# S5 scan: GpSimd instead of VectorE takes the whole turns from the phases

## The chip, the cores and the metric

The kernel runs on one core of one Trainium2 chip. The metric is the device time of one execution in microseconds (us), from the hardware. Engines are named TensorE (PE in the profile, its weight loads PEld), VectorE (DVE), ScalarE (ACT), GpSimd (POOL) and SyncE (SP).

## The reference, cut to what matters

The program is a two-layer backbone: in layer 0 grouped-query attention beside a gated recurrent scan, in layer 1 latent attention beside an S5 diagonal state-space model, and in each layer a mixer that picks and weighs experts. The change touches only the S5 part of layer 1:

```python
for d in range(2):                                   # forward, backward
    lam  = lax.complex(a_re[d], a_im[d])
    dt   = jnp.exp(log_dt[d])[:, None]
    abar = jnp.exp(lam * dt)                         # complex decay, one per state
    ...
    h_ctx = _diag_scan(abar, einsum('btgc,gpc->btgp', fl(ucg), bbar), None)
    h_lat = _diag_scan(abar, einsum('btgc,gpc->btgp', fl(u), bbar), h_ctx[:, -1])
    y = y + fl(einsum('gcp,btgp->btgc', cmat, h_lat).real)
```

There are 256 context positions and 512 latent positions, so each scan is over 768 positions, for 32 groups of 64 states in two directions. All of it is float32.

## The kernel before, in words

Each stage of the kernel is a block of its own, with one instruction stream per engine, and a stage begins when the one before has ended on all engines. The S5 scan (`stage_s5_scan`, L2321 to L2505) handles 128 states at a time: 32 units in all, one for each of 16 pairs of groups and each direction, forward and backward by turns.

The complex scan is made of two real ones. The input of every position is turned back by the angle that the state has run through up to there, then a scan with the real decay (`rate`) alone runs over the real and the imaginary part, and the result is turned forward again. For that a unit needs a sine and a cosine of 768 angles in each of 128 partitions. The steps of unit n, by engine:

- **ScalarE**, `phases(n)`, L2401 and L2404: the time index times the unit's turns per step gives `phase`; the same plus a large constant (`ROUND`, 1.5 times two to the 23rd) gives `whole`, which is the phase rounded to a whole number with the constant still on it. `phase` has two buffers, `whole` has one. ScalarE calls `phases(n+1)` ahead of the sine and cosine of unit n; it first waits until phase n is finished, since only then `whole` is free, and until the cosine of unit n-1 has been read from the other buffer.
- **VectorE**, `phases(n)`, L2441: one instruction, (`whole` - ROUND) - `phase`, leaves the fraction of a turn in `phase`, with its sign turned. It is issued for unit n+1 ahead of the work on unit n.
- **ScalarE**, L2418 to L2423: sine, cosine of half the angle, its square, and the cosine from it. Ahead of them it waits for the finished phase, and (from the third unit on) for the products of unit n-2, since `sin` and `cos` have two buffers.
- **TensorE**, L2364: eight matmuls put the unit's real and imaginary input into PSUM. They start when VectorE has read the input of the unit before (L2468).
- **VectorE**, L2463 to L2466: four products of `sin` or `cos` (SBUF) with the inputs (PSUM); L2469 and L2470: two sums, all operands in SBUF; then the scans over `v` with the broadcast `rate`: L2478 twice on 768 columns in a forward unit, L2480 twice on 256 and L2486 twice on 512 in a backward one.
- **GpSimd**, L2504: four products of the scan's result with `cos` or `sin` over the 512 latent positions, all in SBUF, once the scans of the unit have ended.
- **TensorE**, L2376: eight matmul records take these products to the output in PSUM; after every eight units VectorE reads a quarter of it (L2447).

Beside this ScalarE, TensorE and SyncE work off a piece of the modulation weights in each unit (L130 to L161), which needs neither VectorE nor GpSimd. SyncE issues one load per unit for that. GpSimd issues no transfer in this stage.

The order on each engine is the written one, and semaphores count the units: `phase_rounded` (ScalarE has written `whole`), `phase_ready` (the fraction is there), `trig_ready`, `bu_ready`, `scanned`, `prods_ready`, `y_ready`.

Of the kernel before, what the change touches and what calls it, by code (L numbers as in the profile page):

```python
# [17 lines left out]
ALU = mybir.AluOpType  # L18
# [2148 lines left out]
ROUND = 1.5 * 2.0 ** 23  # L2167
# [153 lines left out]
def stage_s5_scan(nc, g, u_t, rate, turns, b_t, c_t, z_t, later):  # L2321
# [5 lines left out]
    units = [(j, i, d) for j in range(4) for i in range(4) for d in range(2)]  # L2327
    with ExitStack() as stack:
        a = Arena(nc, stack)
        tau = a.sb("tau", [P, 2, T])  # L2330
        phase = a.sb("phase", [P, 2, T])
        whole = a.sb("whole", [P, T])
# [5 lines left out]
        prods = a.sb("prods", [P, 2, 4, LAT])  # L2338
        to_whole = a.sb("to_whole", [P, 1])
        (loaded, rounding_ready, phase_made, phase_rounded, phase_ready, half_ready, sq_ready, trig_ready, bu_ready, bu_used, scanned, prods_ready, y_ready,  # L2340
         y_read, own_v, phase_used, d_added) = a.sem(
            "loaded", "rounding_ready", "phase_made", "phase_rounded", "phase_ready", "half_ready", "sq_ready", "trig_ready", "bu_ready", "bu_used", "scanned",
            "prods_ready", "y_ready", "y_read", "own_v", "phase_used", "d_added")
        mod = ModPiece(a, g, later, [a.sb("ada_ring", [P, DK, P])], 4 * BANK, 5 * BANK, P)
        block = a.block()
        ps = g.ps
# [2 lines left out]
        @block.sync  # L2349
        def _(sp):  # L2350
            sp.dma_start(tau[:], g.d["k_s5_tau"]).then_inc(loaded, 16)
            for j in range(mod.n):
                mod.load(sp, j)
# [78 lines left out]
        @block.vector  # L2432
        def _(dve):
            mod.clear(nc, dve)
            own = Steps(dve, own_v)
            tt = nc.vector.tensor_tensor

            def phases(n):

                dve.wait_ge(phase_rounded, n + 1)  # L2440
                nc.vector.scalar_tensor_tensor(out=phase[:, n % 2], in0=whole[:], scalar=ROUND, in1=phase[:, n % 2],  # L2441
                                               op0=ALU.subtract, op1=ALU.subtract).then_inc(phase_ready, 1)

            def readout(j):
                dve.wait_ge(y_ready, 8 * (j + 1))
                at = VEC["s5_d"][0] + j
                nc.vector.scalar_tensor_tensor(out=z_t[:, j], in0=u_t[:, j, CTX:T], scalar=g.vec[:, at:at + 1],  # L2447
                                               in1=ps[:, YB + (j % 2) * BANK:YB + (j % 2 + 1) * BANK],
                                               op0=ALU.mult, op1=ALU.add).then_inc(y_read, 1)
                dve.wait_ge(y_read, j + 1)  # L2450
                dve.sem_inc(d_added, 1)

            nc.vector.memset(to_whole[:], ROUND).then_inc(rounding_ready, 1)
            phases(0)
            for n, (j, i, d) in enumerate(units):
                unit = d * S5_TILES + 4 * j + i
                b = n % 2
                if n + 1 < len(units):
                    phases(n + 1)
                re, im = ps[:, BU:BU + T], ps[:, BU + 1024:BU + 1024 + T]  # L2460
                dve.wait_ge(trig_ready, n + 1)
                dve.wait_ge(bu_ready, n + 1)
                own(tt(v[:, 0], cos[:, b], re, ALU.mult))  # L2463
                own(tt(x2[:, 0], sin[:, b], im, ALU.mult))
                own(tt(v[:, 1], cos[:, b], im, ALU.mult))
                own(tt(x2[:, 1], sin[:, b], re, ALU.mult))  # L2466
                own.settle()
                dve.sem_inc(bu_used, 1)  # L2468
                own(tt(v[:, 0], v[:, 0], x2[:, 0], ALU.add))  # L2469
                own(tt(v[:, 1], v[:, 1], x2[:, 1], ALU.subtract))  # L2470
                own.settle()
                if n >= 2:
                    dve.wait_ge(prods_ready, n - 1)
                r = rate[:, unit:unit + 1]
                for part in range(2):
                    x, out = v[:, part], s[:, b, part]
                    if d == 0:
                        own(nc.vector.tensor_tensor_scan(out, r.to_broadcast([P, T]), x, 0.0, ALU.mult, ALU.add))  # L2478
                    else:
                        own(nc.vector.tensor_tensor_scan(out[:, 0:CTX][:, ::-1], r.to_broadcast([P, CTX]),  # L2480
                                                         x[:, 0:CTX][:, ::-1], 0.0, ALU.mult, ALU.add))
                if d == 1:
                    own.settle()
                    for part in range(2):
                        x, out = v[:, part], s[:, b, part]
                        own(nc.vector.tensor_tensor_scan(out[:, CTX:T][:, ::-1], r.to_broadcast([P, LAT]),  # L2486
                                                         x[:, CTX:T][:, ::-1], out[:, 0:1], ALU.mult, ALU.add))
                own.settle()
                dve.sem_inc(scanned, 1)  # L2489
                if i == 0 and d == 1 and j:  # L2490
                    readout(j - 1)
            readout(3)
            mod.keep(nc, dve)

        @block.gpsimd
        def _(pool):
            for n in range(len(units)):
                b = n % 2
                pool.wait_ge(scanned, n + 1)
                pool.wait_ge(trig_ready, n + 1)  # L2500
                if n >= 2:
                    pool.wait_ge(y_ready, n - 1)
                for c, (part, table) in enumerate(((0, cos), (1, sin), (0, sin), (1, cos))):
                    last = nc.gpsimd.tensor_tensor(prods[:, b, c], s[:, b, part, CTX:T], table[:, b, CTX:T], ALU.mult)  # L2504
                last.then_inc(prods_ready, 1)  # L2505
# [186 lines left out]
def layer_odd(nc, g, until):  # L2692
    w_in = g.d["od_w_in"][0].rearrange("(k p) n -> p k n", p=P)
    with ExitStack() as stack:
        a = Arena(nc, stack)
        y_t = a.sb("y_t", [P, DK, LAT])
        with ExitStack() as inner:
# [35 lines left out]
            if until >= 9:  # L2733
                N = 2 * S5_TILES
                z_t = y_t[:, 4:DK]
                with ExitStack() as scope:
                    c = Arena(nc, scope)
                    rate = c.sb("rate", [P, N])
                    turns = c.sb("turns", [P, N])
                    b_t = c.sb("b_t", [P, 2, N, P])  # L2740
                    c_t = c.sb("c_t", [P, 3, N, P])
                    stage_s5_parameters(nc, g, rate, turns, b_t, c_t)
                    stage_s5_scan(nc, g, u_t, rate, turns, b_t, c_t, z_t, [(1, u) for u in range(16, 48)])
                w = b.sb("w_out_odd", [P, DK, D])
                w_out = g.d["od_w_out"][0]
                rows = [(slice(0, P), k, w_out[k * P:(k + 1) * P, :]) for k in range(DK)]
                stage_s5_glu(nc, g, z_t, w, rows)
                if until >= 10:
                    stage_mix_out(nc, g, 1, y_t, CTX, w)
# [60 lines left out]
```

## Time and profile before

| what | us |
|---|---|
| runs of the kernel before, median of 3 | 5373.76 |
| lowest and highest of them | 5368.46 and 5385.42 |
| the profiled execution, its own time | 5372.74 |
| its span in the profile | 5370.9 |
| the whole kernel: PE, DVE, ACT, POOL busy | 4356.5, 3626.4, 1193.6, 1541.8 |
| stretch 3380 to 3757 us (this stage), DVE busy | 348.07 of 377 |
| the same stretch, POOL busy | 180.10 of 377 |

The profile gives one execution; its own time is 1.8 us above its span (what lies around the first and last instruction). The shares of the whole kernel are averages over stages with different limits; this stage is about 7% of the span and is read by itself. The granted TensorE clock was 0.86 of full speed in it.

### The profile page before, as it was taken

To read this page: it belongs to the slowest core of one execution; us is meant where nothing else is said; L and a number is where in the kernel's file an instruction comes from. 1 tells how busy PE (TensorE), PEld (TensorE's weight loads), DVE (VectorE), ACT (ScalarE), POOL (GpSimd) and SP (SyncE) were. 2 spreads that over 40 slices of the span, in tenths; PEclk is the share of its full clock that TensorE was granted. 3 is DMA by queue.
4 is the path that set the end of the run, shared out by engine and by line. 5 is a ranking of instruction groups with operands and counts; after the bars stand their busy time and mean duration, and the time that the engine had idled before them with its cause. 6 is when DMAs were issued, how large, how long until landed. Compare 5 with 4: busy or idle time off the path is not lost. (4 is left out here: it accounts for less than half of the span.)

```text
span 5370.9 us, 58089 instructions
## 1 busy us (share of the span) xinstructions
PE 4356.5 (81%) x21260; PEld 3212.1 (60%) x21260; DVE 3626.4 (68%) x6899; ACT 1193.6 (22%) x1919; POOL 1541.8 (29%) x1488
## 2 busy tenths in 40 slices
PE   6976787989999995788788676677689998967886
PEld 5854786865666663454455434333577887856765
DVE  3146764249989887688788534898339988735665
ACT  2125222122232221000000224544223333300000
POOL 0000330004333545344444000354003334333441
PEclk8988898999999997899899878888899999988987
DMA  4211002149888999999999100111238999999996
GB/s 158 63 65 67 1 5 79 48 179 332 284 277 311 413 395 386 366 394 393 378 389 392 54 18 9 42 47 44 79 131 311 315 340 395 366 361 402 403 403 238
DMA packets 465030, 1252.88 MB, mean 233 GB/s; under 512 B 52054, under 2 KB 186956, under 8 KB 459116
## 3 DMA queue, kind: packets, MB, share of 16 engines
q0 software_dynamic: 184320, 671.17, 32.7%
q1 hardware_dynamic: 275984, 569.51, 29.1%
q10 hardware_dynamic: 4444, 8.48, 0.4%
q8 instruction: 171, 2.80, 0.2%
q14 instruction: 111, 0.91, 0.1%
HBM read 1146.24 MB, written 102.76 MB: 233 GB/s over the span
## 5 line engine op out<-in xcount | busy, mean ns | idle before, releaser
L1898 PE MATMUL banks<-acts_in,v_rows 128*128 128x384 f32 (+1 forms) x4096 | 1160.1, 447 | 304.0 <-DMA v_rows<-peer_v 157.2
L1553 PE MATMUL banks<-h_dense,u_t 128*128 128x384 f32 (+1 forms) x4096 | 1216.0, 441 | 0.0
L1898 PEld LDWEIGHTS banks<-acts_in,v_rows 128*128 128x128 f32 x4096 | 798.5, 197 | 665.3 <-DMA v_rows<-peer_v 173.4
L1527 POOL DMA_INDIRECT rows<-peer_u,expert x640 | 655.0, 1024 | 1538.7 <-DVE weight L1798 833.4
L1553 PEld LDWEIGHTS banks<-h_dense,u_t 128*128 128x128 f32 x4096 | 757.1, 195 | 252.0 <-issue 12.2
L1880 POOL DMA_INDIRECT v_fetched<-peer_v,expert x640 | 607.2, 949 | 861.8 <-DVE banks L1958 709.4
L1798 DVE CUSTOM_DVE_ANT_0 rows<-rows,banks 128x1024 f32<-128x1024 f32 x640 | 762.1, 1214 | 128.1 <-DMA rows<-peer_u,expert 80.4
L1958 DVE SCALAR_TENSOR_TENSOR banks<-v_fetched,weight,banks 128x1024 f32<-128x1024 f32 x630 | 784.7, 1283 | 0.0
L1936 DVE TENSOR_TENSOR acts_in<-acts_in,gates 128x384 f32<-128x384 f32 (+1 forms) x256 | 125.1, 489 | 405.1 <-DMA acts_in<-activations 404.9
L1544 PE MATMUL banks<-ident,u_raw 128*128 128x128 f32 x2048 | 319.6, 280 | 82.8 <-DMA u_raw<-peer_u 82.4
L1611 ACT COPY u_t<-banks 128x512 f32<-128x512 f32 x512 | 300.7, 588 | 338.2 <-PE banks L1544 333.8
L1544 PEld LDWEIGHTS banks<-ident,u_raw 128*128 128x128 f32 x2048 | 253.8, 145 | 174.4 <-DMA u_raw<-peer_u 108.2
L1889 ACT COPY y_tok<-banks 128x1024 f32<-128x1024 f32 x5 | 5.1, 1012 | 1460.6 <-DVE banks L1958 1460.6
L2504 POOL TENSOR_TENSOR prods<-s,cos 128x512 f32<-128x512 f32 x64 | 81.0, 1266 | 622.0 <-DVEq L2489 622.0
L1585 PEld LDWEIGHTS banks<-gate_hot,first_hot 128*128 128x128 f32 x1280 | 176.3, 203 | 80.7 <-issue 52.3
L1585 PE MATMUL banks<-gate_hot,first_hot 128*128 128x128 f32 x1280 | 180.5, 288 | 50.6 <-DVE gate_hot L1781 50.6
L2364 PE MATMUL banks<-u_t,b_t 128*128 128x512 f32 (+1 forms) x256 | 128.2, 661 | 106.4 <-DVEq L2468 105.4
L1010 POOL TENSOR_TENSOR z<-expo,keep_k 128x384 f32<-128x384 f32 x28 | 30.8, 1106 | 596.9 <-ACT expo L986 596.9
L1618 ACT ACTIVATE acts<-banks 128x384 f32<-128x384 f32 (+1 forms) x256 | 111.8, 437 | 382.1 <-PE banks L1553 382.0
L1634 ACT COPY part<-banks 128x512 f32<-128x512 f32 x160 | 93.6, 585 | 437.3 <-PE banks L1585 437.3
L1781 DVE TENSOR_SCALAR gate_hot<-iota,slots 128x128 f32<-128x128 f32 x640 | 177.9, 360 | 0.0
L1942 DVE SCALAR_TENSOR_TENSOR x_t<-banks,mod,x_t 128x384 f32<-128x384 f32 (+1 forms) x264 | 160.0, 609 | 0.0
(398 smaller groups left out, 6199.4 us busy)
## 6 DMA issues: line engine op xcount, KB each, us to landing
u_raw<-peer_u SPq DMA_DIRECT2D x256, 512.0 KB, 6.6
v_rows<-peer_v SPq DMA_DIRECT2D x256, 512.0 KB, 15.2
gate_table<-part SPq DMA_DIRECT2D x20, 2048.0 KB, 11.9
activations<-acts SPq DMA_DIRECT2D x128, 192.0 KB
gates<-gate_table SPq DMA_DIRECT2D x8, 3072.0 KB, 22.5
acts_in<-activations SPq DMA_DIRECT2D x128, 192.0 KB, 11.3
peer_wq_in<-peer_wq SPq DMA_DIRECT2D x16, 1024.0 KB, 5.8
ada_ring<-ada_w SPq DMA_DIRECT2D x32, 512.0 KB, 3.8
```

What stands on the lines that cost most here:

```text
L1527: pool.indirect_dma_start(out=ring[:, s % U_RING, :], out_offset=None, in_=rows_of_u, in_offset=bass.IndirectOffsetOnAxis(ap=expert[:, t, ...
L1544: last = nc.tensor.transpose(ps[:, TURN + c:TURN + c + P], u_raw[:, i % 2, c:c + P], g.ident[:])
L1553: last = nc.tensor.matmul(out, u_t[:, i % 2, k * P:(k + 1) * P], h[:, k], start=(k == 0), stop=(k == DK - 1))
L1585: last = nc.tensor.matmul(out[:, j * P:(j + 1) * P], first_hot[:, q % HOTS, j], gate_hot[:, q % HOTS, j], start=True, stop=True)
L1611: nc.scalar.copy(u_t[:, i % 2, c:c + BANK], ps[:, TURN + c:TURN + c + BANK]).then_inc(ut_ready, 1)
L1781: last = nc.vector.tensor_scalar(gate_hot[:, b, j], iota[:], slots[:, 1, c + j:c + j + 1], slots[:, 2, c + j:c + j + 1], ALU.is_equal, ALU ...
L1798: nc.vector.tensor_tensor_reduce(out=row, in0=row, in1=ps[:, H:H + D], scale=1.0, scalar=0.0, op0=ALU.mult, op1=ALU.add, accum_out=weight[ ...
L1880: pool.indirect_dma_start(out=ring[:, s % V_RING, :], out_offset=None, in_=rows_of_v, in_offset=bass.IndirectOffsetOnAxis(ap=expert[:, t, ...
L1898: return nc.tensor.matmul(y_at(m if RESIDENT else j // GROUP * DK + m), v[:, j % V_ROWS, m * P:(m + 1) * P], acts[:, j % V_ROWS], start=st ...
L1942: nc.vector.scalar_tensor_tensor(out=x, in0=y_at(u), scalar=g.mod[:, layer, 40 + m, stream:stream + 1], in1=x, op0=ALU.mult, op1=ALU.add). ...
L1958: last = nc.vector.scalar_tensor_tensor(out=acc(k % 2), in0=row, scalar=weight[:, t, k:k + 1], in1=acc(k % 2), op0=ALU.mult, op1=ALU.add)
L2364: last = nc.tensor.matmul(ps[:, BU + part * 1024 + lo:BU + part * 1024 + hi], b_t[:, part, unit], u_t[:, j, lo:hi], start=True, stop=True)
```

## The change

GpSimd calls `phases` in place of VectorE. Its form has two instructions: a subtraction of the constant from `whole` in place, a wait for that to have landed, and the difference of `whole` and `phase`. GpSimd calls it for units 0 and 1 at the start, and for unit n+2 ahead of its wait for the scans of unit n. VectorE's instruction and its wait for `phase_rounded` are gone. A semaphore that nothing used gives its place to the one of GpSimd's new wait.

```diff
@@ stage_s5_scan
-         y_read, own_v, phase_used, d_added) = a.sem(
+         y_read, own_v, own_p, d_added) = a.sem(
...
@@ block.vector
-            def phases(n):
-
-                dve.wait_ge(phase_rounded, n + 1)
-                nc.vector.scalar_tensor_tensor(out=phase[:, n % 2], in0=whole[:], scalar=ROUND, in1=phase[:, n % 2],
-                                               op0=ALU.subtract, op1=ALU.subtract).then_inc(phase_ready, 1)
-
...
-            phases(0)
             for n, (j, i, d) in enumerate(units):
                 unit = d * S5_TILES + 4 * j + i
                 b = n % 2
-                if n + 1 < len(units):
-                    phases(n + 1)
...
@@ block.gpsimd
+            def phases(n):
+                pool.wait_ge(phase_rounded, n + 1)
+                nc.gpsimd.tensor_scalar(whole[:], whole[:], ROUND, None, ALU.subtract).then_inc(own_p, 1)
+                pool.wait_ge(own_p, n + 1)
+                nc.gpsimd.tensor_tensor(phase[:, n % 2], whole[:], phase[:, n % 2], ALU.subtract)\
+                    .then_inc(phase_ready, 1)
+
+            phases(0)
+            phases(1)
             for n in range(len(units)):
                 b = n % 2
+                if n + 2 < len(units):
+                    phases(n + 2)
                 pool.wait_ge(scanned, n + 1)
```

## Rows read from the trace of the kernel before

**Rows 1.** Page head; 335 us: PE, PEld, DVE, ACT, POOL busy, clock, DMA, GB/s.

```profile
span 5370.9 us, 58089 instructions
...
3400.00:3735.00 335.00, 242.77 (x1007) 119.52 (x1006) 324.19 (x302) 158.11 (x206) 170.22 (x120) 0.88 0.16 48
```

**Rows 2.** Groups by line, 3360 to 3780 us: busy, mean ns | idle before, releasers.

```profile
L2504 POOL TENSOR_TENSOR prods<-s,sin 128x512 f32<-128x512 f32 x64 | 101.7, 1607 | 0.0
L2504 POOL TENSOR_TENSOR prods<-s,cos 128x512 f32<-128x512 f32 x64 | 81.0, 1266 | 622.0 <-DVEq L2489 622.0
...
L2441 DVE SCALAR_TENSOR_TENSOR phase<-whole,phase 128x768 f32<-128x768 f32 x32 | 61.3, 1916 | 12.3 <-ACT whole L2404 7.9
L2478 DVE TENSOR_TENSOR_SCAN s<-rate,v 128x768 f32<-128x768 f32 x32 | 54.5, 1745 | 0.6
...
L2486 DVE TENSOR_TENSOR_SCAN s<-rate,s,v 128x512 f32<-128x512 f32 x32 | 39.4, 1272 | 0.6
...
L2463 DVE TENSOR_TENSOR v<-cos,banks 128x768 f32<-128x768 f32 x32 | 30.1, 942 | 2.6 <-ACT cos L2423 2.3 <-PE banks L2364 0.3
...
L2421 ACT ACTIVATE cos<-cos 128x768 f32<-128x768 f32 x32 | 27.0, 843 | 1.0
...
L2480 DVE TENSOR_TENSOR_SCAN s<-rate,v 128x256 f32<-128x256 f32 x32 | 20.4, 679 | 0.6
```

**Rows 3.** Waits of the same stretch: us in total, times, longest.

```profile
PE banks L2364 <- DVEq L2468: 105.4, 31, 13.2
```

**Rows 4.** Timeline, GpSimd, one unit: start us, us, engine, line.

```profile
3513.65 1.27 POOL L2504 TENSOR_TENSOR prods<-s,cos 128x512 f32<-128x512 f32 x1 [5.42 <-DVEq L2489]
3514.87 3.23 POOL L2504 TENSOR_TENSOR prods<-s,sin 128x512 f32<-128x512 f32 x2
3518.06 1.27 POOL L2504 TENSOR_TENSOR prods<-s,cos 128x512 f32<-128x512 f32 x1
```

**Rows 5.** Timeline, VectorE, the same unit, and the start two units on.

```profile
3513.66 2.07 DVE L2441 SCALAR_TENSOR_TENSOR phase<-whole,phase 128x768 f32<-128x768 f32 x1
3515.65 0.94 DVE L2463 TENSOR_TENSOR v<-cos,banks 128x768 f32<-128x768 f32 x1
...
3518.25 0.94 DVE L2466 TENSOR_TENSOR x<-sin,banks 128x768 f32<-128x768 f32 x1
3519.34 0.96 DVE L2469 TENSOR_TENSOR v<-v,x 128x768 f32<-128x768 f32 x1
3520.21 0.95 DVE L2470 TENSOR_TENSOR v<-v,x 128x768 f32<-128x768 f32 x1
...
3536.20 2.07 DVE L2441 SCALAR_TENSOR_TENSOR phase<-whole,phase 128x768 f32<-128x768 f32 x1
```

**Rows 6.** Timeline of the last unit, which has no L2441 before it.

```profile
3739.08 1.27 POOL L2504 TENSOR_TENSOR prods<-s,cos 128x512 f32<-128x512 f32 x1 [5.43 <-DVEq L2489]
3739.24 0.95 DVE L2463 TENSOR_TENSOR v<-cos,banks 128x768 f32<-128x768 f32 x1 [0.30 <-PE banks L2364]
...
3742.78 1.26 POOL L2504 TENSOR_TENSOR prods<-s,cos 128x512 f32<-128x512 f32 x1
3742.94 1.92 DVE L2469 TENSOR_TENSOR v<-v,x 128x768 f32<-128x768 f32 x1
```

**Rows 7.** One stage of layer 0: VectorE and GpSimd, two SBUF inputs each.

```profile
582.58 2.13 POOL L1013 TENSOR_TENSOR hg<-expo,hg 128x768 f32<-128x768 f32 x1
...
583.53 2.00 DVE L1044 TENSOR_TENSOR expo<-cum 128x768 f32<-128x768 f32 x1
```

**Rows 8.** Lines L1010, L1017: duration ns min/median/max, first and last start, forms.

```profile
L1010 POOL TENSOR_TENSOR z<-expo,keep_k x28: 979/1002/1532, 535.7 to 740.9; 128x384 f32<-128x384 f32 x28
...
L1017 POOL TENSOR_TENSOR k_dec<-expo,keep_k x8: 1799/1800/1801, 554.5 to 782.2; 128x768 f32<-128x768 f32 x8
```

**Rows 9.** The stage's start: the first phases on VectorE.

```profile
3385.69 0.96 DVE L2441 SCALAR_TENSOR_TENSOR phase<-whole,phase 128x768 f32<-128x768 f32 x1 [5.92 <-ACT whole L2404]
3388.62 0.96 DVE L2441 SCALAR_TENSOR_TENSOR phase<-whole,phase 128x768 f32<-128x768 f32 x1 [1.97 <-ACT whole L2404]
3391.84 0.95 DVE L2463 TENSOR_TENSOR v<-cos,banks 128x768 f32<-128x768 f32 x1 [2.26 <-ACT cos L2423]
```

More of the change, by code:

```diff
@@ L2340, in stage_s5_scan @@
         (loaded, rounding_ready, phase_made, phase_rounded, phase_ready, half_ready, sq_ready, trig_ready, bu_ready, bu_used, scanned, prods_ready, y_ready,
-         y_read, own_v, phase_used, d_added) = a.sem(
+         y_read, own_v, own_p, d_added) = a.sem(
             "loaded", "rounding_ready", "phase_made", "phase_rounded", "phase_ready", "half_ready", "sq_ready", "trig_ready", "bu_ready", "bu_used", "scanned",
-            "prods_ready", "y_ready", "y_read", "own_v", "phase_used", "d_added")
+            "prods_ready", "y_ready", "y_read", "own_v", "own_p", "d_added")
         mod = ModPiece(a, g, later, [a.sb("ada_ring", [P, DK, P])], 4 * BANK, 5 * BANK, P)
```

## The prediction

> **What bounds the kernel now.** Stages follow one another, so what this stage gains or loses goes into the time unshortened. I read the page first for the span, then the busy times of the stage's steady stretch. There VectorE is busy 324 of 335 us, GpSimd 170, ScalarE 158 and TensorE 243 [rows 1]: the stage looks bound by VectorE. The groups by line agree: VectorE waited 2.6 us in all ahead of L2463, the first use of sine, cosine and inputs, and TensorE waited 105 us for VectorE to give its inputs free [rows 2, 3]. By this reading the change takes a 2 us step off the bound and should gain.
>
> The timeline shows what the busy times hide. L2441 has a record of 2.07 us beside GpSimd's first product, but 0.96 us at the start of the stage, where GpSimd is idle [rows 5, 9]. GpSimd's next two products take 3.23 us where two others take about 2 x 1.23 [rows 4, 6]. So the two engines did not run side by side: GpSimd's first product (3513.65, 1.23 us to the next start), then VectorE's L2441 (about 0.87), and only then GpSimd's second. In the last unit L2469 comes 0.16 us after the start of GpSimd's fourth product and takes 1.92 us instead of 0.96 [rows 5, 6]. In layer 0 a VectorE instruction of 768 columns with both operands in SBUF takes 2.00 us beside a GpSimd product [rows 7]. But L2463 and L2466, which read one operand from PSUM, keep 0.94 us while GpSimd works [rows 4, 5]. What these rows have in common: a VectorE instruction with two SBUF inputs and a GpSimd product exclude each other for their whole length. I call what they share the port.
>
> The port's load per unit before is: four products of 1.23 us (3739.08 to 3742.78 is three of them [rows 6]), 4.93; L2441, 0.87 (the spacing of three such instructions from 3515.65 to 3518.25 [rows 5]); L2469 and L2470, 1.74; and the scans, if they need it too, (54.5 + 39.4 + 20.4) / 32 = 3.57 [rows 2]. The sum is 11.11 us. A unit takes (3536.20 - 3513.66) / 2 = 11.27 us [rows 5]. The port would be taken all the time but 0.16 us, and VectorE's busy time of 324 us contains its waits for it.
>
> **Does a scan need the port?** No row has a scan beside a GpSimd instruction: GpSimd's products end at about 3519.3, where L2469 begins, and return only when the scans are over [rows 4, 5]. A scan reads two tensors from SBUF, `v` and the broadcast `rate`, so it belongs by its operands with L2441, L2469 and L1044, which were held up, and not with L2463. I take it that it needs the port. The Trainium skill states this for such operands (SBUF — State Buffer, Who interferes with whom): a VectorE instruction with two SBUF inputs contends with a GpSimd instruction that reads SBUF, and the later one waits for the whole of the other. By that rule the time is my forecast; with the scans exempt it is one of the first two rivals.
>
> **The change part by part.**
> - Removed from VectorE: L2441, a slot of 1.99 us (3513.66 to 3515.65 [rows 5]), of which 0.87 is its own port time and the rest is waiting for a product that GpSimd has to do anyway. Of the 32 slots, those for units 2 to 31 lie between two units. The first two lie in ScalarE's lead at the start [rows 9].
> - Added to GpSimd, second instruction: a difference of two tensors of 768 columns. L1017 is exactly that: 1.80 us [rows 8].
> - Added to GpSimd, first instruction: one tensor less a constant, 768 columns. No row shows this on GpSimd. From 384 to 768 columns a product with two inputs goes from 1.00 to 1.80 us [rows 8], so 0.20 is fixed and 1.60 is for 768 columns of two inputs. With one input I take half: 0.20 + 0.80 = 1.00 us. Low end: 0.84 us, what ScalarE takes for 768 columns of one input [rows 2]. High end: 1.80 us, the second input costing nothing. A gain is excluded, since the instruction is new. The Trainium skill (GPSIMD Engine Reference, Engine selection) says one-input work on GpSimd runs roughly at line rate and two-input work about twice as slow; at its 1.2 GHz that is 0.64 + 0.20 = 0.84 us, which would take 5 us off the sum.
> - The wait between the two (own_p): some 0.1 us, during which VectorE has the port; it costs only at the start. Behind it stand the unit's products, and TensorE's output and ScalarE's sine of two units on behind these.
> - "Two units ahead" gives no lead by itself. ScalarE writes `whole` for unit n+2 only after phase n+1 is finished, as before. But by the time GpSimd is through with the products of unit n-1 it has done so, hence GpSimd's wait for it costs nothing. No transfer moves.
>
> **Where it lies in a unit.** Scans of a unit end; GpSimd starts its four products and VectorE its four instructions on PSUM, which need no port. Then L2469, L2470 and the scans, 5.3 us, meet the rest of the products and the new pair, and each waits for the other in turn. VectorE's scans are the end of the chain, so all of it adds up: 4.93 + 1.74 + 3.57 + 1.00 + 1.80 = 13.04, and the same 0.16 us of handing over: 13.20 us per unit against 11.27, **1.93 us more**. It is the same as 1.00 + 1.80 - 0.87: the port carries 2.80 us of new work for 0.87 of old.
>
> **The sum.** In units 1 to 29 a phase pair and four products lie beside VectorE's work: 29 x 1.93 = 56.0. In unit 0 only the pair does; one wait for its first instruction, 1.0. Unit 30 has lost L2441 and has no pair any more: it gives back 1.99 and waits for one product, 1.24: -0.8. At the start the first phase takes 1.00 + 0.1 + 1.80 instead of 0.96, and ScalarE's next step waits for it: +1.9. Unit 31 stays as it is. In all +58.1 us. The profiled execution took 5372.74, its span 5370.9; that gives 5430.8. The median of the runs is 1.0 us above it, and I take **5431**.
>
> What covers the rest, and is late next: sine and cosine of unit n+2 begin after the products of unit n, some 6 us into a unit, take about 3.4 us (four steps like L2421 [rows 2]) and are done before 10, so they stay hidden in 13.2 us. TensorE waited 105 us over 31 units, 3.4 each [rows 3], and waits longer.
>
> **Rivals.**
> - **Scans don't need the port, L2469 goes ahead of the fourth product (faster).** This is the case on the other side. Then the pair runs beside the scans for nothing. VectorE's unit is 11.27 - 1.99 = 9.28, and it waits for one product of 1.24 in front of L2469 or L2470: 10.52, or 0.75 less per unit. 29 x -0.75, with start, unit 0 and unit 30 (1.9 + 1.0 - 0.8): -20, 5354. It decides if a scan keeps its 1.75 us while GpSimd works. For it: scans are another kind of instruction, at half the speed, and no row holds one beside GpSimd. Against: their operands.
> - **Scans don't need it, the fourth product goes first.** L2469 is ready 3.69 us after VectorE's first product (3515.65 to 3519.34), the fourth product starts 3.70 after GpSimd's first [rows 5, 6], a tie. If the product wins, L2469 waits 1.24 and L2470 waits 1.00 for the new subtraction: 9.28 + 2.24 = 11.52, 0.25 more, 29 x 0.25 + 2.1 = +9: 5383, no difference that counts. In my forecast the tie changes nothing, since all the work has to pass the port.
> - **GpSimd's subtraction costs as much as two inputs.** The port carries 0.80 more: 58 + 30 x 0.80 = +82: 5456.
> - **The busy times are right after all**, L2441's slot falls away and nothing comes for it: 30 x -1.99 = -60, 5314. Against it stands the last unit, the one without L2441 already: its L2469 took 0.96 longer [rows 6].
>
> **How the numbers follow.** A measurement of this kernel can tell about 0.3%, 16 us, from no change. Chances: forecast with the subtraction anywhere from 0.84 to 1.5 us, 0.77; subtraction at about 1.80 or more, 0.08; scans free and faster by 20 us, 0.09; scans free and about level, 0.05; the full gain, 0.01. So faster 0.10, same 0.05, slower 0.85. The range takes the port case: at the low end 0.16 x 30 = 5 us less for the subtraction and about as much again if the handing over of 0.16 a unit goes, 5420, and 3 us for the spread of runs: 5417. At the high end the price of 1.80 gives 5456. The two cases with free scans are left out, 15 in 100.
>
> **What would show it.** L2441 is gone; GpSimd has 32 subtractions of about 1.0 us and 32 differences of 1.8 us or, where they waited, more. L2478, L2480 and L2486 rise: their sum goes from 114 us to about 114 + 30 x 2.8 less what falls to L2470, so L2478's mean is well over 2 us. L2470 and L2469 together wait about 1.2 us or more per unit. VectorE still looks busy over 90% of the stage, its distance from unit to unit is about 13.2 us, and the stage is 58 us longer. I am wrong if L2478 keeps 1.75 us with a GpSimd record beside it; then the unit is 10.5 to 11.5 us. If the scans wait and the time still is elsewhere, it is the subtraction's own length.

## The result and the profile after

The changed kernel took 5414.91 us (median of 4 runs, 5413.85 to 5433.23) where the kernel before took 5376.95 in the runs beside it (5368.46 to 5385.42). The ratio is 1.0076, 95% interval 1.0059 to 1.0092: slower by 38 us, clear of noise. I had forecast 5431, +58 us. The direction and the mechanism held. My +58 us is half as large again as the +38 us measured, and the median lies 2 us below the low end of my range, 5417.

Line numbers move: L2463 is now L2454, L2469 and L2470 are L2460 and L2461, the scans L2478, L2480, L2486 are L2469, L2471, L2477, and GpSimd's products L2504 are L2506. New are L2490 (GpSimd's subtraction of the constant) and L2492 (its difference). The page's head and the same 335 us of the stage, which answer to [rows 1]:

```profile
span 5413.3 us, 58123 instructions
...
3400.00:3735.00 335.00, 242.57 (x905) 117.29 (x906) 323.37 (x242) 143.94 (x188) 265.25 (x159) 0.81 0.15 43
```

VectorE is busy for 323 of 335 us, as before (324), and gets through fewer instructions in them (242 against 302). The granted TensorE clock was 0.81 of full speed here against 0.88. VectorE waited for TensorE only once in this stage, 10.5 us at its end, and before it was 11.5 us in the same place, so the clock is not where the time went.

VectorE's and GpSimd's groups of the stage (line, engine, operation, tiles, shapes, count | busy us, mean ns | idle before, releasers), which answer to [rows 2]:

```profile
L2490 POOL TENSOR_SCALAR whole<-whole 128x768 f32<-128x768 f32 x32 | 88.7, 2772 | 434.3 <-ACT whole L2404 434.3
...
L2469 DVE TENSOR_TENSOR_SCAN s<-rate,v 128x768 f32<-128x768 f32 x32 | 77.9, 2477 | 0.5
L2492 POOL TENSOR_TENSOR phase<-whole,phase 128x768 f32<-128x768 f32 x32 | 72.3, 2260 | 2.7
...
L2460 DVE TENSOR_TENSOR v<-v,x 128x768 f32<-128x768 f32 x32 | 59.5, 1860 | 4.7
L2461 DVE TENSOR_TENSOR v<-v,x 128x768 f32<-128x768 f32 x32 | 48.4, 1513 | 0.0
...
L2471 DVE TENSOR_TENSOR_SCAN s<-rate,v 128x256 f32<-128x256 f32 x32 | 44.8, 1442 | 0.5
L2477 DVE TENSOR_TENSOR_SCAN s<-rate,s,v 128x512 f32<-128x512 f32 x32 | 39.4, 1272 | 0.6
L2454 DVE TENSOR_TENSOR v<-cos,banks 128x768 f32<-128x768 f32 x32 | 30.5, 954 | 22.4 <-ACT cos L2423 15.2 <-DVE s L2469 3.9 <-DVE s L2477 2.7
```

The two sums before, which [rows 2] leave out:

```profile
L2469 DVE TENSOR_TENSOR v<-v,x 128x768 f32<-128x768 f32 x32 | 31.6, 988 | 4.7
L2470 DVE TENSOR_TENSOR v<-v,x 128x768 f32<-128x768 f32 x32 | 30.4, 952 | 0.0
```

L2441's 61.3 us [rows 2] are gone from VectorE, and still it is as busy: the two sums and the scans took 176.3 us and now take 270.0, 93.7 more. Their work is the same as before; I read the growth as waiting for the port, and the timeline below shows it. L2454, which reads one operand from PSUM, has kept its length. Apart from the 15.2 us at the start, nothing of VectorE's idle time grew by more than 0.22 us a unit.

One forward unit, VectorE and then GpSimd, from the timeline:

```profile
3499.14 1.99 DVE L2460 TENSOR_TENSOR v<-v,x 128x768 f32<-128x768 f32 x1
3501.05 1.57 DVE L2461 TENSOR_TENSOR v<-v,x 128x768 f32<-128x768 f32 x1
3502.66 4.97 DVE L2469 TENSOR_TENSOR_SCAN s<-rate,v 128x768 f32<-128x768 f32 x2
...
3511.55 1.99 DVE L2460 TENSOR_TENSOR v<-v,x 128x768 f32<-128x768 f32 x1
```

```profile
3499.05 1.27 POOL L2506 TENSOR_TENSOR prods<-s,cos 128x512 f32<-128x512 f32 x1
3500.28 2.84 POOL L2490 TENSOR_SCALAR whole<-whole 128x768 f32<-128x768 f32 x1
3503.20 2.82 POOL L2492 TENSOR_TENSOR phase<-whole,phase 128x768 f32<-128x768 f32 x1
3507.77 1.27 POOL L2506 TENSOR_TENSOR prods<-s,cos 128x512 f32<-128x512 f32 x1 [1.75 <-DVEq L2480]
```

Read it as one queue for the port. L2460 comes 0.09 us behind the fourth product and waits for it (1.99 instead of 0.96). GpSimd's subtraction then waits for L2460. L2461 waits for the subtraction, 1.57 instead of 0.95: 0.62 us. The difference, L2492, waits for the first scan (2.82 instead of 1.81), and the second scan waits for the difference: the pair takes 4.97 instead of 3.41. The shortest, the median and the longest of the single scans show that one of a pair waits and the other does not:

```profile
L2469 DVE TENSOR_TENSOR_SCAN s<-rate,v x32: 1728/1760/3308, 3401.8 to 3781.3; 128x768 f32<-128x768 f32 x32
```

So **a scan does need the port**: it waits for GpSimd's difference, and the difference waits for a scan. The trace of before had no row on this. From one L2460 to the next are 12.41 us. GpSimd then idles 1.75 us until the scans end, so it is not the bound by its own load.

What was mis-sized shows at the start of the stage, where VectorE has nothing to do yet:

```profile
3387.08 2.13 POOL L2490 TENSOR_SCALAR whole<-whole 128x768 f32<-128x768 f32 x1 [430.27 <-ACT whole L2404]
3389.29 1.80 POOL L2492 TENSOR_TENSOR phase<-whole,phase 128x768 f32<-128x768 f32 x1
3393.11 2.13 POOL L2490 TENSOR_SCALAR whole<-whole 128x768 f32<-128x768 f32 x1 [2.02 <-ACT whole L2404]
```

The subtraction alone takes 2.13 us, longer than the difference of two tensors, and above the 1.80 that I had as its high end. Yet it keeps VectorE waiting for 0.62 us only. I call this wait the hold. It is counted from the start of the waiting instruction, so the true hold can be a few hundredths of a us longer.

**Where the 42 us are.** The profiled execution took 5415.21 us, 42.5 more than that of before. From the first to the last L2463 (now L2454), 31 units, it was 3391.84 to 3739.24 before [rows 6, 9], 347.4 us, and is now:

```profile
L2454 DVE TENSOR_TENSOR v<-cos,banks x32: 953/954/956, 3396.3 to 3783.6; 128x768 f32<-128x768 f32 x32
```

387.3 us, so 39.9 more, or as an average of the 31 units 12.49 us against 11.21. The two ends of the stage are in this average. Between them a forward and a backward unit together take 25.22 us, 12.61 each, against 11.27 before [rows 5]:

```profile
3734.97 0.95 DVE L2454 TENSOR_TENSOR v<-cos,banks 128x768 f32<-128x768 f32 x1 [0.22 <-DVE s L2469]
...
3747.79 0.95 DVE L2454 TENSOR_TENSOR v<-cos,banks 128x768 f32<-128x768 f32 x1 [0.22 <-DVE s L2477]
...
3760.19 0.95 DVE L2454 TENSOR_TENSOR v<-cos,banks 128x768 f32<-128x768 f32 x1 [0.22 <-DVE s L2469]
```

The units 1 to 29, counted from one L2454 to the next, make 39.0 of the 39.9 us, or 1.345 each; units 0 and 30 together make the other 0.9. The first phases at the start take 3.1 more: the first L2463 came 12.29 us after the stage's first VectorE instruction (3379.55), L2454 comes 15.39 after it (3380.88). The stages ahead make 1.3 us and what lies behind the last L2454 makes -1.9. The average between first and last start is the measure of each experiment below, called "a unit" there.

### The profile page after: what moved, and what is told of

Same layout as the page of the kernel before. It is cut to its first block and busy times, and to the rows that moved or that the text cites. A ratio compares the mean times of both kernels' runs of the same rounds, so it can differ in the third digit from the quotient of the medians.

```text
span 5413.3 us, 58123 instructions
## 1 busy us (share of the span) xinstructions
PE 4365.0 (81%) x21260; PEld 3208.7 (59%) x21260; DVE 3660.3 (68%) x6867; ACT 1193.0 (22%) x1919; POOL 1680.8 (31%) x1552
## 5 line engine op out<-in xcount | busy, mean ns | idle before, releaser
L2364 PE MATMUL banks<-u_t,b_t 128*128 128x512 f32 (+1 forms) x256 | 149.6, 754 | 125.9 <-DVEq L2459 125.0
L2490 POOL TENSOR_SCALAR whole<-whole 128x768 f32<-128x768 f32 x32 | 88.7, 2772 | 434.3 <-ACT whole L2404 434.3
L1010 POOL TENSOR_TENSOR z<-expo,keep_k 128x384 f32<-128x384 f32 x28 | 30.8, 1105 | 598.0 <-ACT expo L986 598.0
L2364 PEld LDWEIGHTS banks<-u_t,b_t 128*128 128x128 f32 x256 | 71.3, 292 | 190.8 <-DVEq L2459 128.3
```

Of the source, the lines that this page charges most:

```text
L2364: last = nc.tensor.matmul(ps[:, BU + part * 1024 + lo:BU + part * 1024 + hi], b_t[:, part, unit], u_t[:, j, lo:hi], start=True, stop=True)
```

## The experiments

**Does GpSimd's work beside the scans cost VectorE time, and by what?** Three runs put one spare GpSimd instruction into the kernel before, where the change has its pair, and differ in it alone.

```diff
             for n in range(len(units)):
                 b = n % 2
+                if n >= 2:
+                    pool.wait_ge(y_ready, n - 1)
+                spare = prods[:, b].rearrange("p c t -> p (c t)")[:, 0:T]
+                if n:
+                    nc.gpsimd.tensor_tensor(spare, tau[:, 0], tau[:, 1], ALU.mult).then_inc(phase_used, 1)    # e1
+                    nc.gpsimd.tensor_scalar(spare, tau[:, 0], 2.0, None, ALU.subtract).then_inc(phase_used, 1)  # e2
+                    nc.gpsimd.memset(spare, 0.0).then_inc(phase_used, 1)                                        # e3
                 pool.wait_ge(scanned, n + 1)
                 pool.wait_ge(trig_ready, n + 1)
-                if n >= 2:
-                    pool.wait_ge(y_ready, n - 1)
+                if n:
+                    pool.wait_ge(phase_used, n)
```

> The kernel before, with one more GpSimd instruction in each of 31 units, after the four products: the product of two constant tensors of 768 columns, written where the next products will overwrite it. Nobody waits for it. Port theory (VectorE instructions with two SBUF inputs, scans among them, and GpSimd instructions that read SBUF exclude each other): L2470 and the scans are held by about 1.6 us per unit, as the first scan pair was in the changed kernel, so 31 x 1.6 = +50 us; L2478 or L2480 rise. Rival 'scans are free': it runs beside the scans, at most L2470 is held, +0 to 10 us.

> As the run before, but the spare instruction subtracts a constant from one tensor of 768 columns. Its record should be 2.13 us, as that of the changed kernel beside nothing. Port theory with the hold read from the changed kernel (VectorE was held 0.62 us by an instruction of 2.13 us): 31 x 0.65 = +20 us. Rival 'the record's whole length is what VectorE waits for': 31 x 2.1 = +66 us, more than the difference costs. By my prediction's price of 1.00: +31 us.

> As the run before, but the spare instruction only writes: a memset of 768 columns. Port theory for reads: nothing is held, 0 us within 0.1%, records of L2470 and the scans as before. Rival 'any GpSimd work in this place holds VectorE': its record's length of under 1 us per unit, up to +25 us.

The product of two tensors gave 1.0093 (1.0070 to 1.0117), +50 us; the subtraction 1.0034 (1.0022 to 1.0045), +18 us; the memset 1.0004 (0.9993 to 1.0015), nothing. From the groups by line, e1, e2 and e3 in turn:

```profile
L2469 DVE TENSOR_TENSOR v<-v,x 128x768 f32<-128x768 f32 x32 | 80.3, 2509 | 4.7
...
L2503 POOL TENSOR_TENSOR prods<-tau 128x768 f32<-128x768 f32 x31 | 56.9, 1836 | 0.0
```

```profile
L2503 POOL TENSOR_SCALAR prods<-tau 128x768 f32<-128x768 f32 x31 | 85.9, 2770 | 0.1
...
L2469 DVE TENSOR_TENSOR v<-v,x 128x768 f32<-128x768 f32 x32 | 61.5, 1922 | 4.7
...
L2470 DVE TENSOR_TENSOR v<-v,x 128x768 f32<-128x768 f32 x32 | 47.8, 1494 | 0.0
...
L2441 DVE SCALAR_TENSOR_TENSOR phase<-whole,phase 128x768 f32<-128x768 f32 x32 | 32.4, 1013 | 12.4 <-ACT whole L2404 8.0
```

```profile
L2469 DVE TENSOR_TENSOR v<-v,x 128x768 f32<-128x768 f32 x32 | 31.7, 990 | 4.7
L2470 DVE TENSOR_TENSOR v<-v,x 128x768 f32<-128x768 f32 x32 | 30.4, 951 | 0.0
...
L2503 POOL MEMSET prods<- 128x768 f32 x31 | 22.8, 737 | 0.0
```

A record of 1.84 us costs 50 us and one of 2.77 us costs 18, so the length of GpSimd's record is not what VectorE pays. In e3, GpSimd writes 768 columns beside L2469 in each unit, and L2469 keeps its 0.99 us: this write alone held nobody up. In e1 the hold fell on L2469, not on L2470 and the scans as I had written. In e2 L2469 is longer too (1.92 against 0.99), but that is an old wait in a new place: L2441 got the port ahead of GpSimd's first product there and fell from 1.92 to 1.01 us, and L2469 waited for the fourth product instead. What is new is the 0.54 us more on L2470. The scans kept their length in all three runs, so these runs do not bear on whether a scan needs the port; the timeline of the changed kernel does. Per unit (first to last L2463): 12.77 us in e1, 11.78 in e2, 11.20 in e3, against 11.21.

**What was L2441 worth?**

```diff
-                dve.wait_ge(phase_rounded, n + 1)
-                nc.vector.scalar_tensor_tensor(out=phase[:, n % 2], in0=whole[:], scalar=ROUND, in1=phase[:, n % 2],
-                                               op0=ALU.subtract, op1=ALU.subtract).then_inc(phase_ready, 1)
+                pass
...
-                    act.wait_ge(phase_ready, n)
+                    act.wait_ge(phase_rounded, n)
...
-                act.wait_ge(phase_ready, n + 1)
+                act.wait_ge(phase_rounded, n + 1)
```

> Leaves out the subtraction of the whole turns altogether (sine and cosine are taken of the unreduced phase); ScalarE still writes both tensors. It prices what the change took from VectorE. Port theory: of L2441's slot of 1.99 us the 0.87 of its own goes, the wait for a product moves to L2469 or L2470 (last unit of the kernel before: 0.96): 30 x -0.9 = -27 us. Rival 'VectorE's busy time is the bound': 30 x -1.99 = -60 us.

0.9947 (0.9926 to 0.9968), -26 us by the medians (5350.50 against 5376.40); 10.37 us a unit. The sine and cosine are then taken of the unreduced phase, so this is a price and not a kernel to keep. It is the most that taking L2441 off VectorE could bring with all else left as it is, since nothing is put in its place. Of its slot of 1.99 us the port part goes and the wait for a product moves to the next instruction on the port (now L2467):

```profile
L2467 DVE TENSOR_TENSOR v<-v,x 128x768 f32<-128x768 f32 x32 | 59.8, 1868 | 4.7
```

**Is it a matter of where L2441 waits?** The kernel before, with `phases(n + 1)` called behind the first product instead of ahead of it:

```diff
-                if n + 1 < len(units):
-                    phases(n + 1)
...
                 own(tt(v[:, 0], cos[:, b], re, ALU.mult))
+                if n + 1 < len(units):
+                    phases(n + 1)
                 own(tt(x2[:, 0], sin[:, b], im, ALU.mult))
```

> The kernel before with L2441 issued behind L2463 instead of ahead of it, nothing else. It then reaches the port 0.87 us into GpSimd's first product and its wait of 1.1 us shrinks to about 0.2. Rival 'what bounds is the wait in that one place': 30 x -0.85 = -25 us. Port theory: the port was taken already for 11.1 of 11.27 us; GpSimd's products still end late and L2469 waits for the fourth instead, so the time stays within 0.2% of the kernel before.

1.0002 (0.9993 to 1.0012). L2441's mean falls from 1.92 to 1.14 us and L2469's rises from 0.99 to 1.59:

```profile
L2469 DVE TENSOR_TENSOR v<-v,x 128x768 f32<-128x768 f32 x32 | 50.9, 1589 | 4.7
...
L2441 DVE SCALAR_TENSOR_TENSOR phase<-whole,phase 128x768 f32<-128x768 f32 x32 | 36.6, 1144 | 6.0 <-ACT whole L2404 6.0
```

Of a wait of 0.77 us that was taken away in one place, 0.60 came back in another, and a unit takes 11.13 us where it took 11.21. This is how a shared resource that is almost full looks.

**The changed kernel without GpSimd's subtraction.** ScalarE takes the constant off.

```diff
-                nc.scalar.activation(whole[:], phase[:, n % 2], ACT.Identity, bias=to_whole[:])\
-                    .then_inc(phase_rounded, 1)
+                nc.scalar.activation(whole[:], phase[:, n % 2], ACT.Identity, bias=to_whole[:]).then_inc(own_p, 1)
+                act.wait_ge(own_p, n + 1)
+                nc.scalar.activation(whole[:], whole[:], ACT.Copy, bias=-ROUND).then_inc(phase_rounded, 1)
...
-                nc.gpsimd.tensor_scalar(whole[:], whole[:], ROUND, None, ALU.subtract).then_inc(own_p, 1)
-                pool.wait_ge(own_p, n + 1)
```

> The changed kernel, but ScalarE takes the constant off `whole` (one more ScalarE instruction per unit, about 0.9 us, with 0.1 us of its own wait), and GpSimd only forms the difference. Port theory with the measured holds: GpSimd's subtraction held VectorE 0.62 us per unit, so 30 x 0.62 = 19 us off the changed kernel, and 2 to 3 us off its start: about 5394 where the changed kernel has 5415, and still 18 us above the kernel before, because a difference of about 1.6 us on the port stands for VectorE's 0.87. Rival 'the subtraction's 2.13 us record is in the chain': 60 us off, below the kernel before.

1.0049 (1.0035 to 1.0064) of the kernel before, 5398.58 against 5372.66 us: 11.91 us a unit, 18.1 us over 31 units below the changed kernel and 21.8 above the kernel before. The subtraction's share is 0.58 us a unit, not 2.13. What is left is the difference, which holds VectorE's L2462 (the former L2470) for 2.57 - 0.95 = 1.62 us where VectorE's own instruction took 0.87 of the port. GpSimd and VectorE, from the timeline of this run:

```profile
3543.20 2.53 POOL L2491 TENSOR_TENSOR phase<-whole,phase 128x768 f32<-128x768 f32 x1
```

```profile
3543.98 2.57 DVE L2462 TENSOR_TENSOR v<-v,x 128x768 f32<-128x768 f32 x1
```

**The pair ahead of the products.**

```diff
-                if n + 2 < len(units):
-                    phases(n + 2)
                 pool.wait_ge(scanned, n + 1)
+                if n + 2 < len(units):
+                    phases(n + 2)
                 pool.wait_ge(trig_ready, n + 1)
```

> The changed kernel with GpSimd's pair ahead of the four products of a unit instead of behind them: the same instructions in another order. The rival that only the sum of the holds on the port counts expects the time of the changed kernel within 0.2%. My reading is that the port is held 0.62 us of the subtraction's 2.13 us; ahead of the products GpSimd wastes the rest of it in the 3.5 us in which VectorE needs no port, and the products then fall beside L2469, L2470 and the scans. Per unit: pair until 4.0 us, the products from there; about 1 us more than now, 25 to 40 us above the changed kernel.

1.0155 (1.0137 to 1.0172): 13.75 us a unit, 39 us over the changed kernel. The same instructions in another order take longer, so the sum of the holds alone does not set the time. My reading was that a pair in the stretch in which VectorE wants no port wastes that stretch. This run does not show it by itself: the products now end so late that ScalarE's sine and cosine come late as well, a wait that I had called covered. Waits of this run, in total, times, longest:

```profile
DVE v L2454 <- ACT cos L2423: 73.2, 17, 15.1
```

Without the 15.1 at the start these are 16 waits of 3.6 us, 58 us in all, which is more than the 39 us lost. How much of the loss is wasted port time and how much is late sine and cosine stays open. The order in the change, pair behind products, is the better of the two.

**Taking load off the port.** If the port bounds, VectorE's instruction should be made to use one SBUF operand. In e7, 512 of the 768 columns of `whole` lie in PSUM; in e9, all of them, for which the output has one bank instead of two.

```diff
# e7
-        whole = a.sb("whole", [P, T])
+        whole = a.sb("whole", [P, 256])
...
+        whole_ps = ps[:, 3 * BANK:4 * BANK]
...
-                nc.scalar.activation(whole[:], phase[:, n % 2], ACT.Identity, bias=to_whole[:])\
+                nc.scalar.activation(whole_ps, phase[:, n % 2, 0:BANK], ACT.Identity, bias=to_whole[:])
+                nc.scalar.activation(whole[:], phase[:, n % 2, BANK:T], ACT.Identity, bias=to_whole[:])\
...
-                nc.vector.scalar_tensor_tensor(out=phase[:, n % 2], in0=whole[:], scalar=ROUND, in1=phase[:, n % 2],
+                nc.vector.scalar_tensor_tensor(out=phase[:, n % 2, 0:BANK], in0=whole_ps, scalar=ROUND,
+                                               in1=phase[:, n % 2, 0:BANK], op0=ALU.subtract, op1=ALU.subtract)
+                nc.vector.scalar_tensor_tensor(out=phase[:, n % 2, BANK:T], in0=whole[:], scalar=ROUND,
+                                               in1=phase[:, n % 2, BANK:T],
                                                op0=ALU.subtract, op1=ALU.subtract).then_inc(phase_ready, 1)
```

```diff
# e9; the packing of the inputs is in e7 too
-        whole = a.sb("whole", [P, T])
...
+        whole = ps[:, 3 * BANK:3 * BANK + T]
...
-        mod = ModPiece(a, g, later, [a.sb("ada_ring", [P, DK, P])], 4 * BANK, 5 * BANK, P)
+        mod = ModPiece(a, g, later, [a.sb("ada_ring", [P, DK, P])], 5 * BANK, 7 * BANK, P)
...
-                    for lo, hi in halves(T):
-                        last = nc.tensor.matmul(ps[:, BU + part * 1024 + lo:BU + part * 1024 + hi],
+                    for lo, hi in (((0, 512), (512, T)) if part == 0 else ((0, 256), (256, T))):
+                        last = nc.tensor.matmul(ps[:, BU + part * T + lo:BU + part * T + hi],
...
-                if i == 0 and d == 0 and j >= 2:
-                    pe.wait_ge(y_read, j - 1)
-                out = ps[:, YB + (j % 2) * BANK:YB + (j % 2 + 1) * BANK]
+                if i == 0 and d == 0 and j >= 1:
+                    pe.wait_ge(y_read, j)
+                out = ps[:, YB:YB + BANK]
```

> The kernel before, with 512 of the 768 columns of `whole` in a PSUM bank of their own (the inputs are packed into three banks for it), 256 still in SBUF; L2441 becomes two instructions. Port theory: the instruction on 512 columns reads one operand from SBUF and runs beside GpSimd's first product; the one on 256 waits for that product's end and holds the port 0.3 us. Its slots are about 1.45 us in all instead of 1.99, and L2469 starts when the fourth product ends: a unit of about 10.6 us instead of 11.27, 30 x -0.65 = -20 us, faster than both kernels. Rival 'VectorE's own work is the bound': one more instruction on it, +0.1 us per unit, +3 us.

> The kernel before with all 768 columns of `whole` in PSUM (inputs packed into three banks, one output bank instead of two, so TensorE waits for VectorE's read of the output after each eight units). Port theory: L2441 stays one instruction on VectorE but reads only `phase` from SBUF and runs beside GpSimd's first product, record 0.94; L2469 waits about 0.3 us for the fourth product; a unit of 10.4 us, 30 x -0.85 = -25 us, or up to 9 us less of a gain if the three waits for the output bank are not covered. Rival 'VectorE's own busy work is the bound, L2441 costs its own 0.87': no change, 0 us, or the three waits.

e7: 0.9980 (0.9970 to 0.9989), 10.82 us a unit, -12 us over the 31 units where I had written -20. The two slots were 1.47 us as expected, so 0.52 less than 1.99 and not 0.65: my sum was off there, not the wait. That makes 16 us. The other 4 went where VectorE reads the output between two units, three times: the two units around such a reading take as long as others in the kernel before, and 1.2 us longer in e7. e9: 0.9962 (0.9949 to 0.9976), 5350.89 against 5373.99 us, **20 us faster than before by the ratio (23 by the medians) and some 60 below the changed kernel**; 10.43 us a unit. Its timeline, GpSimd and VectorE at the start of a unit:

```profile
3539.19 1.27 POOL L2504 TENSOR_TENSOR prods<-s,cos 128x512 f32<-128x512 f32 x1 [5.62 <-DVEq L2489]
3540.42 2.50 POOL L2504 TENSOR_TENSOR prods<-s,sin 128x512 f32<-128x512 f32 x2
```

```profile
3539.20 0.96 DVE L2441 SCALAR_TENSOR_TENSOR phase<-banks,phase 128x768 f32<-128x768 f32 x1
3540.08 0.94 DVE L2463 TENSOR_TENSOR v<-cos,banks 128x768 f32<-128x768 f32 x1
...
3543.76 1.21 DVE L2469 TENSOR_TENSOR v<-v,x 128x768 f32<-128x768 f32 x1
```

In what these two engines do it is the picture of [rows 4, 5] with one thing changed: the same instruction on the same engine, in the same place, reads one operand from PSUM, and takes 0.96 us beside the product instead of 2.07; the next two products take 2.50 instead of 3.23. The edit also moved the inputs and the output in PSUM; the waits that this brought fall on TensorE, 7.7 us in the whole stage, and VectorE did not wait for them in its products:

```profile
PE banks L2376 <- DVE y_t L2447: 7.7, 3, 3.6
```

## Why the prediction was right, and where its size was off

- **The bound.** Right: not VectorE's busy time but what it shares with GpSimd. e4 took 26 us where the busy time promised 60, and e8 moved a wait without moving the time.
- **Scans need the port.** It was argued from their operands and is now shown by the timeline after (up to 3.31 us instead of 1.75 for the scan that waits). Both rivals with free scans fall with it.
- **The difference.** I priced it at 1.80 us, its record; it holds the port 1.62 (e5; in e1 a product of the same size does the same to L2469, 2.57 us instead of 0.96).
- **The subtraction** is the term that was mis-sized. I took 1.00 us as record and hold in one. Its record is 2.13 us, its hold 0.62. My rival with 1.80 us was nearer to the record and wrong on what it would do: it forecast 5456. With the measured holds the step of the prediction gives 0.62 + 1.62 - 0.87 = 1.37 us a unit where I had 1.93, and 29 x 1.37 = 39.7; the trace shows 39.0 for these 29 units. This is also why the median fell below my range: its low end still had 0.84 us for the subtraction and 1.80 for the difference.
- **Handing over.** The port's load becomes 4.93 + 1.74 + 3.57 + 0.62 + 1.62 = 12.48 us. The average of 12.49 meets it only by chance, since it holds the shorter units at the two ends; a unit between them takes 12.61, so 0.13 is left over, near the 0.16 us that I had added. The same sum in the other runs, against the mean of two neighbouring units in their timelines: before 11.11 against 11.27, e4 and e9 10.24 against 10.40, e2 11.73 against 11.86, e5 11.86 against 12.02, e1 12.73 against 12.89. A remainder of 0.13 to 0.16 us in seven kernels whose units go from 10.4 to 12.9 us is the best support that the account has. It is not a measured cost of handing over: the sum counts GpSimd's products by their spacing, 1.23 us, while a product held VectorE for 1.11 (2.07 - 0.96). The sum does not hold for e6, and in e8 nothing is left over (11.12).
- **Page and trace.** The Trainium skill (GPSIMD Engine Reference, Engine selection) calls one-input work roughly line rate. The record of 2.13 us says otherwise. The hold of 0.62 us fits it: 768 elements at the 1.2 GHz of that page's Specifications are 0.64 us, an estimate. The Trainium skill (SBUF — State Buffer, Who interferes with whom) has the loser wait for the whole instruction. That agrees with e1 nearly (1.62 of 1.80 us) and not with e2 (0.62 of 2.13); and it leaves out a GpSimd instruction that only writes, which e3 agrees with (1.0004).
- **The start.** Forecast +1.9 us, measured +3.1; the subtraction's 2.13 instead of 1.00 is that difference.
- **The tie of L2469 and the fourth product** went to the product in most units and did not matter, as said. **The cover of sine and cosine** held in the changed kernel (the cosine was ready 4.1 us before L2454 in the unit shown); in e6 it did not.

## What to carry to other kernels

Before work is moved from VectorE to GpSimd, look at the records of VectorE's instructions with two SBUF inputs while GpSimd reads SBUF: where they are twice as long as alone, the two engines are one resource, and a piece of work should be placed where it holds that resource shortest. Here a fused instruction on VectorE (0.87 us of the port) beat two on GpSimd (0.62 + 1.62). What helped was to put one operand in PSUM, at the price of an output bank; that was tried on this one instruction only.

## What the runs showed of the hardware that I had not expected

- A GpSimd subtraction of a constant from 768 float32 columns takes 2.13 us alone, a product or difference of two tensors of that size 1.80. In place or not makes no difference in the runs (2.77 and 2.77 us as means beside VectorE).
- The record and the hold differ: VectorE was held 0.62 us by the first and 1.62 by the second. The record of such a GpSimd instruction is no price for its neighbour.
- A memset of 768 columns on GpSimd takes 0.74 us and did not lengthen L2469 beside it (e3).
- In all timelines shown the two engines took turns at the port: neither got it twice in a row while the other waited. Why, no run here tells.
